# State-space outputs: lag matrices written out in full, three load rooms, state copies shared otherwise

## The reference, cut to what matters

```
_, s = lax.associative_scan(_linear_recurrence, (a, bu), axis=1)
return (jnp.einsum('btgp,ghp->btgh', s.real, c_re.astype(f32))
        - jnp.einsum('btgp,ghp->btgh', s.imag, c_im.astype(f32)))
...
y_lat = yf[:, t_ctx:] + jnp.flip(yb[:, t_ctx:], 1) + d * ul
```

## Time and profile before

| | us |
|---|---|
| median of 3 runs (lowest to highest) | 2591.81 (2591.51 to 2593.81) |
| the profiled execution, whole | 2592.18 |
| its span, first to last instruction | 2590.6 |
| end of the scan | 1951.85 |
| first output product | 1954.83 |
| last gelu begins | 2012.95 |
| SP begins the next stage | 2016.57 |

### The profile page before, as it was taken

The page is one execution under the profiler, slowest core; times in us unless marked ns, Lnnn a source line. Parts: engine busy times, 40 slices in busy tenths (PEclk is TensorE's granted clock), DMA queues, the critical chain, the costliest instruction groups (busy, mean ns, idle before and its releaser), DMA issues. The chain is left out here.

```text
span 2590.6 us, 29067 instructions
## 1 busy us (share of the span) xinstructions
PE 2314.7 (89%) x11596; PEld 1867.4 (72%) x11596; DVE 1446.2 (56%) x2138; ACT 699.8 (27%) x862; POOL 745.1 (29%) x439
## 2 busy tenths in 40 slices
PE   5998697798879999999999998898975788999987
PEld 3886586576667777787777786787855667878875
DVE  4663325697638887766676564417893333831223
ACT  4102232476323121222222222305114322111121
POOL 0211111110544655665563221110000451212240
PEclk8999799899899999999999998699997888999998
DMA  6554322232311333333333110144235522111111
GB/s 237 219 199 154 136 89 99 90 114 74 123 65 55 101 108 101 102 112 115 104 109 108 48 42 17 73 143 142 81 107 162 183 106 78 41 49 48 42 41 73
DMA packets 107821, 264.97 MB, mean 102 GB/s; under 512 B 8934, under 2 KB 52358, under 8 KB 104584
## 3 DMA queue, kind: packets, MB, share of 16 engines
q1 hardware_dynamic: 100564, 241.26, 27.8%
q10 hardware_dynamic: 7128, 21.92, 2.2%
HBM read 222.79 MB, written 57.13 MB: 108 GB/s over the span
## 5 line engine op out<-in xcount | busy, mean ns | idle before, releaser
L2339 POOL TENSOR_TENSOR w_lo<-w_staged,w_hi 128x1024 fp32r<-128x1024 f32 x66 | 162.2, 2457 | 404.5 <-ACT w_hi L2431 404.4
L233 POOL TENSOR_TENSOR w_lo<-w_staged,w_hi 128x1024 fp32r<-128x1024 f32 (+1 forms) x34 | 84.0, 2471 | 254.6 <-ACT w_hi L200 254.5
L1261 PE MATMUL ps_in<-h_hi,w_hi 128*128 128x512 f32 x400 | 130.5, 408 | 29.9 <-DVE mixed L1357 20.7
L2481 DVE SCALAR_TENSOR_TENSOR x<-ps_n,mod,x 128x1024 f32<-128x1024 f32 x88 | 112.9, 1283 | 61.1 <-PE ps_n L2373 60.6
L1253 POOL TENSOR_TENSOR w_lo<-w_staged,w_hi 128x1024 fp32r<-128x1024 f32 x23 | 56.8, 2471 | 276.9 <-ACT w_hi L1238 276.9
L2431 ACT CAST w_hi<-w_staged 128x1024 fp32r<-128x1024 f32 x66 | 69.0, 1045 | 218.3 <-PE ps_dn L2373 218.3
L1261 PE MATMUL ps_in<-h_lo,w_hi 128*128 128x512 f32 x400 | 127.4, 400 | 0.0
L1261 PE MATMUL ps_in<-h_hi,w_lo 128*128 128x512 f32 x400 | 126.3, 398 | 0.0
L374 PE MATMUL ps_odd<-o_hi,w_hi 128*128 128x512 f32 x384 | 120.9, 396 | 4.0 <-DVE o_lo L648 4.0
L366 POOL TENSOR_TENSOR w_lo<-w_staged,w_hi 128x1024 fp32r<-128x1024 f32 x24 | 58.1, 2420 | 227.9 <-ACT w_hi L349 227.9
L2481 DVE SCALAR_TENSOR_TENSOR x<-ps_dn,mod,x 128x1024 f32<-128x1024 f32 x88 | 112.9, 1283 | 15.7 <-PE ps_dn L2373 9.3
(11 more groups left out here) (466 smaller groups left out, 5593.6 us busy)
## 6 DMA issues: line engine op xcount, KB each, us to landing
w_staged<-in_w_ff SPq DMA_DIRECT2D x66, 512.0 KB, 3.6
x_ctx<-in_w_ada SPq DMA_DIRECT2D x48, 512.0 KB, 5.2
x_in<-in_w_ada SPq DMA_DIRECT2D x16, 1024.0 KB, 7.8
scratch_bias<-scratch_line ACTq DMA_DIRECT2D x8, 2048.0 KB
att_bias<-scratch_bias SPq DMA_DIRECT2D x32, 512.0 KB, 3.3
w_staged<-in_w_in SPq DMA_DIRECT2D x17, 512.0 KB, 5.1
ada_w<-in_w_ada SPq DMA_DIRECT2D x8, 1024.0 KB, 19.7
scratch_cp<-ff_shared SPq DMA_DIRECT2D x16, 384.0 KB, 5.9
```

Source lines behind the costliest of these rows:

```text
L233: nc.gpsimd.tensor_tensor(st.lo[i % 2][:, 0:widths[i]], st.staged[i % 2][:, 0:widths[i]], st.hi[i % 2][:, 0:widths[i]].bitcast(F32), ALU.s ...
L1261: last = nc.tensor.matmul(ps[i % 2][:, a:a + BANK], u[i % 2][:, k * P:(k + 1) * P], r[:, k, a:a + BANK], start=(k == 0 and part == 0), sto ...
L2339: nc.gpsimd.tensor_tensor(st.lo[i % 2][:, :], st.staged[i % 2][:, :], st.hi[i % 2][:, :].bitcast(F32), ALU.subtract).then_inc(st.split, 1)
L2481: nc.vector.scalar_tensor_tensor(x[:, k, :], ps_dn[k % 2][:, :], gate_f[:, k:k + 1], x[:, k, :], ALU.mult, ALU.add).then_inc(added, 1)
```

## The change

The lag matrices are written out in full. `store_lags` stores, in place of one DMA of 15 blocks, eight DMAs in each batch of the feed-forward layer, one for each lag j, into a new array `scratch_toeplitz`, in the layout of the 128x128 matrix: lags 0 to 2 behind the `bt` store, 3 to 5 in the next weight unit, 6 and 7 in the one after, behind the next batch's `cp` store. `take_taps` waits for all eight. The output stage then loads each batch's lag matrix with one DMA of 384 KB in pieces of 3072 bytes (1024 in the third room).

There are three rooms for loads; the third lies where z and the Fourier input were, so its first load waits for these. SP waits for the products three batches before. The two stores of the Fourier result move behind the load of batch 4. The lag products of batches 0 and 1 are issued right after the Fourier transform, before the states exist, and in each later batch all six come ahead of the twelve state products. ACT copies one of the two lower quarters and DVE three quarters; the folds come behind the copies of batches 2 and 3. The loops on DVE, SP and PE are written out.

The twelve lag products of batches 0 and 1 (L2935) now stand ahead of all state products (L2944). The core of the diff:

```diff
@@ StepMatrices @@
         sp.wait_ge(self.taken, 2 * b + 2)
-        sp.dma_start(self.g.dram["taps"][:, b * MB:(b + 1) * MB, :], self.taps[:, :, :, :].rearrange("p i e h -> p i (e h)")
-                     ).then_inc(self.taps_stored, 16)
+        self.store_lags(sp, b, range(0, 3))
+
+    def store_lags(self, sp, b, lags):
+        groups = slice((b % 2) * MB, (b % 2 + 1) * MB)
+        for j in lags:
+            sp.dma_start(self.g.dram["toeplitz"][b // 2, j * SH:(j + 1) * SH, groups, :],
+                         self.taps[:, :, CT - 1 - j:2 * CT - 1 - j, :].rearrange("p i e h -> p i (e h)")).then_inc(self.taps_stored, 16)
...
-            dve.wait_ge(self.taps_stored, 16 * b)
+            dve.wait_ge(self.taps_stored, 16 * CT * b)
@@ gated_ffn, SP @@
+                if i >= 9 and i % 3 == 0 and (i - 9) // 3 < mats.N:
+                    mats.store_lags(sp, (i - 9) // 3, range(3, 6))
+                if i >= 10 and i % 3 == 1 and (i - 10) // 3 < mats.N:
+                    mats.store_lags(sp, (i - 10) // 3, range(6, CT))
@@ scan_and_outputs @@
-    cp = [free_lo[:, 2 + 2 * s:4 + 2 * s, 0:GB * P].rearrange("p c (i n) -> p c i n", n=P) for s in range(2)]
-    taps = [free_lo[:, 6 + s, 0:GB * P].rearrange("p (i n) -> p i n", n=P) for s in range(2)]
+    cp_room = [free_lo[:, 2 + 2 * s:4 + 2 * s, 0:GB * P] for s in range(2)] + [low[:, 0:2 * GB * P // LC, :]]
+    tap_room = [free_lo[:, 6 + s, 0:GB * P].unsqueeze(1) for s in range(2)] + [u_f[:, 0:GB * P // LC, :]]
+    ROOMS = len(cp_room)
...
-    LOADS = 16 * (CT + 1)
+    LOADS = 32
@@ scan_and_outputs, SP @@
-                for j in range(CT):
-                    a = (CT - 1 - j) * SH
-                    sp.dma_start(taps[s][j * SH:(j + 1) * SH, :, :], g.dram["taps"][:, bass.ds(b * GB, GB), a:a + P]).then_inc(loaded[s], 16)
...
+                sp.dma_start(tap_room[s], g.dram["toeplitz"][b].rearrange("p i n -> p (i n)").rearrange("p (r t) -> p r t", t=tap_room[s].shape[-1])
+                             ).then_inc(loaded[s], 16)
+            load(0)
+            load(1)
+            for s in range(2):
+                sp.wait_ge(z_stored[s], 16 * (KD // 2))
+            sp.wait_ge(by_pe, FNET_IN)
+            load(2)
+            for b in range(ROOMS, N):
+                if b == 5:
+                    for i in range(S):
+                        sp.wait_ge(folded, 3 * (i + 1))
+                        sp.dma_start(g.dram["yf"][i], yf[i]).then_inc(y_stored, 16)
+                sp.wait_ge(done, b - ROOMS + 1)
+                load(b)
@@ scan_and_outputs, PE @@
+            def tap_products(b):
+                s = b % 2
+                pe.wait_ge(loaded[b % ROOMS], LOADS * (b // ROOMS) + LOADS)
+                if b >= 2:
+                    pe.wait_ge(gelued, b - 1)
+                for i in range(GB):
+                    nc.tensor.matmul(ps_b[:, s, i * NLAT:(i + 1) * NLAT], taps_of(b % ROOMS, i), u[:, b * GB + i, NCTX:NC5],
+                                     start=(i % PER_BANK == 0), stop=False)
+
+            def state_products(b):
+                s = b % 2
                 for x in gathered:
                     pe.wait_ge(x, b + 1)
...
+            for b in range(2):
+                tap_products(b)
+            for b in range(N):
+                if b >= 2:
+                    tap_products(b)
+                state_products(b)
@@ scan_and_outputs, ACT @@
-                for c in range(2):
-                    last = nc.scalar.copy(states[s][lower, c, :, :], of(lower, NCTX, b, c))
-                last.then_inc(gathered[0], 1)
+                nc.scalar.copy(states[s][lower, 0, :, :], of(lower, NCTX, b, 0)).then_inc(gathered[0], 1)
@@ scan_and_outputs, DVE @@
+                nc.vector.tensor_copy(states[s][lower, 1, :, :], of(lower, NCTX, b, 1))
                 for c in range(2):
                     last = nc.vector.tensor_copy(states[s][upper, c, :, ::-1], of(upper, NCTX, b, c))
...
-            for i in range(S):
-                fold(i)
-            with dve.Fori(1, N // 2) as turn:
-                gather(turn * 2, 0, turn, False)
-                gather(turn * 2 + 1, 1, turn, False)
+            for b in range(N):
+                gather(b)
+                if 2 <= b < 2 + S:
+                    fold(b - 2)
```

More of the change, by code:

```diff
@@ L2112, in all_stored @@
         sp.wait_ge(self.bt_stored, 16 * self.N)
-        sp.wait_ge(self.taps_stored, 16 * self.N)
+        sp.wait_ge(self.taps_stored, 16 * CT * self.N)
     def make_skip(self, pool):
@@ L2758, in scan_and_outputs @@
         y_stored = ctx.enter_context(nc.semaphore("fnet_stored"))
-        loaded = [ctx.enter_context(nc.semaphore(f"s5_out_loaded{s}")) for s in range(2)]
+        loaded = [ctx.enter_context(nc.semaphore(f"s5_out_loaded{s}")) for s in range(ROOMS)]
         gathered = [ctx.enter_context(nc.semaphore(f"s5_gathered_{d}")) for d in ("fwd", "bwd")]
@@ L2803, in _, with load @@
             sp.dma_start(half_row, g.dram["dft"][HT, 0:1, 0, 0:HALF]).then_inc(dft_loaded, 16)
[L2805 to L2808, removed]
+            def load(b):
+                s = b % ROOMS
+                sp.dma_start(cp_room[s], g.dram["cp"][b].rearrange("p c i n -> p (c i n)").rearrange("p (r t) -> p r t", t=cp_room[s].shape[-1])
                              ).then_inc(loaded[s], 16)
-                for j in range(CT):
-                    a = (CT - 1 - j) * SH
-                    sp.dma_start(taps[s][j * SH:(j + 1) * SH, :, :], g.dram["taps"][:, bass.ds(b * GB, GB), a:a + P]).then_inc(loaded[s], 16)
-            def put_fourier():
-                for i in range(S):
[L2816 to L2823, removed]
+                sp.dma_start(tap_room[s], g.dram["toeplitz"][b].rearrange("p i n -> p (i n)").rearrange("p (r t) -> p r t", t=tap_room[s].shape[-1])
[13 more added lines that the diff above has]
+                load(b)
             for s in range(2):
@@ L2903, in _ @@
             last.then_inc(by_pe, 1)
-            def batch(b, s, turn, first):
-                pe.wait_ge(loaded[s], turn * LOADS + LOADS)
+            PER_BANK = BANK // NLAT
+            def tap_products(b):
[8 more added lines that the diff above has]
+                s = b % 2
                 for x in gathered:
                     pe.wait_ge(x, b + 1)
-                if not first:
-                    pe.wait_ge(gelued, b - 1)
                 for i in range(GB):
[L2912 to L2916, removed]
-                last.then_inc(done, 1)
-            in_pairs(pe, N, batch)
+                    for c in range(2):
+                        last = nc.tensor.matmul(ps_b[:, s, i * NLAT:(i + 1) * NLAT], cp_of(b % ROOMS, c, i), states[s][:, c, i, :],
+                                                start=False, stop=(c == 1 and (i % PER_BANK == PER_BANK - 1 or i == GB - 1)))
+                last.then_inc(done, 1)
+            for b in range(2):
[4 more added lines that the diff above has]
+                state_products(b)
         def half(rows, c, k):
@@ L3030, in _, with gather @@
                     low_part(split_behind[m])
-            def gather(b, s, turn, first):
-                if not first:
+            def gather(b):
+                s = b % 2
+                if b >= 2:
                     dve.wait_ge(done, b - 1)
+                nc.vector.tensor_copy(states[s][lower, 1, :, :], of(lower, NCTX, b, 1))
                 for c in range(2):
@@ L3046, in _ @@
             dve.wait_ge(by_pe, FNET_OUT)
-            gather(0, 0, 0, True)
-            gather(1, 1, 0, True)
             dve.wait_ge(by_act, HT + 6)
-            for i in range(S):
-                fold(i)
-            with dve.Fori(1, N // 2) as turn:
-                gather(turn * 2, 0, turn, False)
-                gather(turn * 2 + 1, 1, turn, False)
+            for b in range(N):
+                gather(b)
+                if 2 <= b < 2 + S:
+                    fold(b - 2)
     st.strips += n
@@ L3182, in build @@
         image_stored = semaphore("bias_image_stored")
+        g.dram["toeplitz"] = nc.dram_tensor("scratch_toeplitz", (GROUPS // GB, P, GB, P), F32).ap()
         g.dram["spill"] = nc.dram_tensor("scratch_spill", (3 * HEADS, P, L), F32).ap()
```

7 lines of the change are left out of this document (added).

## The result

The changed kernel takes 2576.88 us (median of five runs, 2575.51 to 2578.16), the kernel before 2591.81 (2588.91 to 2593.81, also five): a ratio of 0.994, 95% interval 0.9928 to 0.9952. Forecast were 2572.8 us, within 2564 to 2584. The profiled execution took 2576.88 us (span 2575.1), 15.3 less than that of before; forecast were 19.0 less.

| stretch | before, us | after, us | change | forecast |
|---|---|---|---|---|
| start to the first `take_taps` of the feed-forward layer (no changed code runs) | 837.9 | 840.3 | +2.4 | 0 |
| from there to the layer's last gate or value product | 735.1 | 737.5 | +2.4 | +2.0 |
| to the scan's end | 378.8 | 378.7 | -0.1 | 0 |
| outputs: scan's end to the last gelu | 61.1 | 41.6 | -19.5 | -21.0 |
| the rest | 577.7 | 577.0 | -0.7 | 0 |

The account below looks back on a forecast made before the run. The prediction took TensorE's waits for loads in the outputs as the bound, with DMAs still bounding them afterwards. Outputs -21.0 and feed-forward layer +2.0 made -19.0 us, from 2592.18 to 2573.2, 2572.8 as median; range 2564 to 2584.

Parts of the forecast that it names:

- Start of the outputs: Outputs, batch 0: states ready at 1954.2 after three DVE copies (2.3 us), 24 records in 4.2 us, done at 1958.5.
- the first 3.1 us at the slow level: Outputs, batch 0: TensorE runs at its slow clock for only the first 3.1 us, so 24 records take 4.2 us.
- The rate of the DMAs: Outputs: mixed loads and stores flow at 322 GB/s, so 8.5 MB take 26.5 us; ends 390 and 245 GB/s.
- The DMAs bound the stage, with a pause of 0.8 us per batch: Outputs: DMAs set about 4.9 us per batch, later than TensorE's floor, with TensorE pausing some 0.8 us each.
- One pause near batch 5: Outputs: TensorE pauses 2 to 3 us once, where the Fourier stores stand in the queue ahead of batch 5's load.
- pauses of that length should not bring the slow level back: Outputs: TensorE's clock stays at the quick level through pauses of 0.8 us per batch and one of 2 to 3.
- Sum of the outputs: Outputs: batch 7 done at 1992.0 instead of 2012.95, a change of -21.0 us.
- TensorE's 26.9: Outputs after batch 0, TensorE's floor: 2.7 us for batch 1 and 6 x 4.03 for the others.
- quick supply: Rival, outputs: loads keep up at 390 GB/s, TensorE's floor holds, -27.5 us there, 2566.3 us in all; chance 0.20.
- Feed-forward layer: Taps wait for lag stores 6 and 7, delaying TensorE's gate strip in one batch of four: 4 x 0.5 = 2 us.
- batches of the other kind: Feed-forward layer: batches with store and taps 5.1 us apart, not 3.6; taps 1.1 us late, just inside the reserve.
- the lag stores eat it: Rival, feed-forward layer: late landings of lags 6 and 7 delay every batch, 26 us at x = 2.3, 2597 us; chance 0.08.

Follow-up runs that it names:

- e0: The changed kernel run again without edits: 2576.54 us, ratio 0.9938 to the kernel before.
- e4: The changed kernel with two load rooms, and the lag matrices stored by one 15-block DMA and loaded by eight small DMAs, as before: 2590.49 us, ratio 0.9991.
- e10: The changed kernel with all eight lag stores right behind the bt store and the Fourier stores behind the last load: 2570.36 us, ratio 0.9911.
- e11: The changed kernel with all eight lag stores right behind the bt store of their batch, a repeat on another chip: 2574.45 us, ratio 0.993.
- e3: The changed kernel with two rooms for loads instead of three: 2590.71 us, ratio 0.9991.
- e2: The changed kernel with the two Fourier stores behind the last load of the outputs: 2573.39 us, ratio 0.9924.
- e9: The changed kernel with lag stores right behind the bt store, Fourier stores behind the last load, and filler products on TensorE at the scan's end: 2571.12 us, ratio 0.9912.
- e5: The changed kernel with the old state copies (ACT both lower quarters, DVE the two upper ones): 2578.48 us, ratio 0.9945.
- e7: The kernel before with the change's lag stores added in the same places, `take_taps` waiting for them and nothing reading them: 2598.52 us, ratio 1.0019.
- e8: The changed kernel with eleven unread filler products on TensorE while the scan ends: 2576.77 us, ratio 0.9938.

## Why the prediction came out as it did

*Start of the outputs.* Batch 0 was forecast for 6.65 us after the scan's end and was done after 8.0. The states came as computed: TensorE began at 1959.11, 2.5 us after the scan's end (2.3). The failed term is "the first 3.1 us at the slow level": 48 records in 8.09 us are 24 at 0.224 and 24 at 0.112, so all of batch 0 was slow, 5.4 us rather than 4.2. I had read the duration of the slow level from a start after another pause; it is not a constant. In the eight traces of this order of work and these copies (after, e0 to e4, e10, e11) batch 0 is done 7.6 to 8.1 us after the scan's end.

*The rate of the DMAs.* I took 322 GB/s for mixed traffic. Measured were 395 over 21.9 us with loads and output stores mixed, 1 KB pieces included, at a share of 1.03. The windows with less in the earlier trace rows were not poorer because of mixing. The forecast allowed for both readings, and 379 for a full share of large pieces was the closer one. The rule of the Trainium skill (DMA: Bandwidth & Descriptors, Specifications) that 512 bytes is the smallest transfer at line rate is neither borne out nor refuted by after, of which no stretch consists of 512-byte pieces. In e4, with such pieces among the loads, two windows (1963 to 1967) have 343 GB/s at a share of 1.09 and 371 at 1.03, where e3, with large ones, has 415 and 418 at 1.03 and 1.04 (1974.5 to 1976.5): against the rule, though size and number of the DMAs change together there.

*The DMAs bound the stage, with a pause of 0.8 us per batch.* Wrong, as the rate was. After the slow start TensorE ran batches 2 to 4 and 6 and 7 at its own pace, 3.9 to 4.3 us each (batch 1, whose lag products were done, 3.0). The supply only just kept up: the load of batch 3 landed at 1971.3, and its products began then, after a wait of 0.3 us.

*One pause near batch 5.* Right in place and cause, but too small: 2 to 3 us were forecast, 4.36 measured, and it grew by the step that I had called safe, "pauses of that length should not bring the slow level back". It held behind 0.87 us in e2, 1.93 in e9 and 2.87 in e3, but not behind 2.08 in e5; after this one the granted clock fell to 0.58 (the window from 1984.50), and 36 records took 0.84 + 0.94 us more than at the quick level. What the size left out is the wait of SP itself: I counted the Fourier stores as bytes in the queue, and they are also an instruction that waits for DVE's second fold until 1972.7, with the load of batch 5 behind it; that is 1.8 us of its lateness (16.6 us after the scan's end, 14.8 in e2). 4.36 + 1.78 = 6.1 us is what stands ahead of batch 5's end; e2, which moves both bytes and wait away, takes back 5.1 to 5.7.

*Sum of the outputs.* 40.1 us after the scan's end were forecast, 41.6 measured. This is closer than its parts. Beside batch 0 (6.65) and TensorE's 26.9 the forecast had 40.1 - 33.6 = 6.5 us of pauses, spread over the batches and set by the rate; measured were 6.1 us at batch 5 alone, all but some 0.9 of it set by the order of the SP queue (e2 still waits 0.87), and 41.6 - 8.0 - 26.9 - 6.1 = 0.6 elsewhere. The total was right by the wrong cause: at the measured rate and with the pause of 2 to 3 us that I gave batch 5, the same working gives 33.6 + 2 to 3 = 35.6 to 36.6 us, 5 to 6 too low. The rival "quick supply" was right on the rate, but its 33.6 us from the scan's end were reached by no run: e2, without the hole, has 36.5, and e9, with batch 0 quick as well, 36.6.

*Feed-forward layer.* +2.0 us forecast, 2.9 and 4.5 of lost time in two executions. The step was right in detail: the second lag store lands 0.3 us behind `cp`; the taps of batch 2 begin 922.28 - 920.04 = 2.24 us after their products end, where before had 0.18: 2.1 late (1.9 forecast), and TensorE loses 0.85 us (0.6) there; batches 2, 6, 10 and 14 are hit. Mis-sized was the rest: batches of the other kind are over the edge too when their spacing happens to be short (12 in after; 8 in e7, with 1.36 us, the largest). For that kind the forecast was at odds with itself: its own numbers, 5.9 + x - 5.1 - 1.2, give a loss of x - 0.4 us, not the x - 0.9 of the rival. With x = 0.3 that is 0.1 us short of a loss, so a landing a little late is enough. The rival "the lag stores eat it" would by this have needed x = 1.6 rather than 2; measured was 0.3.

*What the sum gained from what.* By undoing one part at a time: the third room 12.9 us, the full matrices as one load 4.5, the early lag products 2.0 to 2.6, together 19.4 to 20.0, and the stage became 19.5 shorter (two profiles of the same kernel differ by 0.6 here). The agreement is in part built in: before, e4, e3 and after are a chain (61.1, 59.0, 54.5, 41.6), and only its first step, 2.1 us, is open to be explained by the early products. The new shares bring nothing, or a loss of up to 1. The lag stores cost 2.9 to 4.6. The medians fell by 14.9 us and the two profiles by 15.3; the parts of one pair of profiles are good to some 2 to 4 us, by which executions differ even where the code is the same.

What stays open: why TensorE is slow for longer in some executions in the stage before the feed-forward layer. The first `take_taps` stood at 837.4 to 841.9 in the 13 profiles with changed code, in 11 of them at 839.2 or later, and at 837.9 in the one of before. Whether before varies as much is not known, since only one execution of it has a profile; so some 2 us of cost of the changed kernels ahead of the layer is not ruled out. From the layer's end to the scan's end, again the same code, the 14 profiles have 376.1 to 380.6 us.

## What to carry to other kernels

A deeper buffer pays as long as the requests themselves aren't late: read a store that sits ahead of a load on one queue as a wait for its producer first, and as bytes second. Small stores are nearly free when they follow their own producer at once, and cost when they are put behind the next round's large store that a consumer then waits for. Both sentences rest on this kernel alone. Check a forecast by its parts before its total: here 6.5 us of pauses from a rate too low looked like 6.1 us of hole, most of it from the order of a queue.

## What the runs showed of the hardware

The DMAs sustained 395 GB/s, single windows of 2 us 417, on one core with loads and stores mixed; the best window of before had 390. When the queue is that full a load lands late: issues of the `cp` pieces in the output stage, with count, size and median us from issue to landing, before and after:

```profile
over_lo<-scratch_cp SPq DMA_DIRECT2D x6, 768.0 KB, 5.6
```

```profile
over_lo<-scratch_cp SPq DMA_DIRECT2D x5, 768.0 KB, 9.3
```

9.3 us are more than two batches of TensorE (2 x 4.03), so with three rooms there is still nothing to spare.

TensorE's granted clock read 1.00 through the 4.36 us of the pause in after, and fell with the work running again (0.58). Pauses of 3.80 us in e8 and 3.87 in e3 brought the slow level back in full (2.93 us for the 12 records behind them), 0.87 and 1.93 us in e2 and e9 did not (1.60). The length of the pause alone doesn't settle it: behind 2.08 us in e5 the next 12 and 24 records took 1.95 and 4.17 us (1.50 and 2.84 at the quick level), and in e3 the 12 records took 2.10 behind one of 1.83 us and 1.60 behind one of 2.87:

```profile
1999.64 2.10 PE L2934 MATMUL ps_strips<-x,over_lo 128*128 128x128 f32 x12 [1.83 <-DMA over_lo<-scratch_toeplitz]
...
2008.42 1.60 PE L2934 MATMUL ps_strips<-x,over_lo 128*128 128x128 f32 x12 [2.87 <-DMA over_lo<-scratch_toeplitz]
```
